# State-space rounds of a hybrid decoder step: inputs and outputs moved on chip instead of through DRAM, tables loaded a round earlier, and the low part moved from GpSimd to VectorE

## The reference

```
u  = h.reshape(L, 64 groups, 16)                 # h = rmsnorm(x)
bu = einsum('gpc,blgc->blgp', bb, u)             # complex, 64 states a group
st = associative_scan(lambda-bar, bu)            # along the 1024 rows
y  = Re(einsum('gcp,blgp->blgc', c, st)) + d * u
y  = gelu(y)
pg = y @ w_glu
out = pg[:, :1024] * sigmoid(pg[:, 1024:])
```

## Time and profile before

| what | value |
|---|---|
| median of 3 runs | 3394.28 us (3385.55 to 3394.67) |
| profiled execution | 3400.61 us |
| its span, first to last instruction | 3398.8 us |
| PE busy | 3170.3 us, 93% |
| DVE, POOL, ACT busy | 1908.5, 869.8, 810.2 us |
| mean granted TensorE clock | 0.96 of full |
| the S5 rounds, from the end of the norm to the first unit of the gate product | 2227 to 2422 us |

### The profile page before, as it was taken

The page is one execution under the profiler, slowest core; times in us unless marked ns, Lnnn a source line. Parts: engine busy times, 40 slices in busy tenths (PEclk is TensorE's granted clock), DMA queues, the critical chain, the costliest instruction groups (busy, mean ns, idle before and its releaser), DMA issues.

```text
span 3398.8 us, 69059 instructions
## 1 busy us (share of the span) xinstructions
PE 3170.3 (93%) x29883; PEld 2989.3 (88%) x29883; DVE 1908.5 (56%) x4225; ACT 810.2 (24%) x1839; POOL 869.8 (26%) x775
## 2 busy tenths in 40 slices
PE   5999999999999999799999999965897999999998
PEld 4879888888888897699999999954897999999997
DVE  5556666666666666587777676376124332333235
ACT  3334444343444343310011100122103100000001
POOL 2202121121212121133333333234231333333331
PEclk8879999999999999899999999977898999999999
DMA  2111222121212111111222222366110111111111
GB/s 97 52 52 54 71 62 62 59 65 53 65 56 68 60 59 61 30 44 53 77 85 71 71 85 73 111 184 185 52 46 25 50 44 51 44 50 44 50 44 63
DMA packets 111326, 223.46 MB, mean 66 GB/s; under 512 B 24880, under 2 KB 59184, under 8 KB 110000
## 3 DMA queue, kind: packets, MB, share of 16 engines
q1 hardware_dynamic: 82400, 177.66, 16.9%
q10 hardware_dynamic: 28624, 41.38, 3.7%
HBM read 177.86 MB, written 41.14 MB: 64 GB/s over the span
## 4 chain that ended last, share of the span: by engine, by line
PE 86%; DVE 9%; ACT 2%; DMA 1%; issue 1%; POOL 1%; SPq 1%; POOLq 0%; DVEq 0%; ACTq 0%
PE ps L223 33%; PE ps L618 16%; PE ps L1361 15%; PE ps L704 5%; PE ps L652 2%; PE ps L239 1%; PE ps L282 1%; PE ps L679 1%; PE ps L645 1%; PE ps L672 1%; PE ps L630 1%; PE ps L685 1%; PE ps L636 1%; DMA tab<-keep_tab 1%; PE ps L1952 1%
## 5 line engine op out<-in xcount | busy, mean ns | idle before, releaser
L223 PE MATMUL ps<-hhi,whi 128*128 128x344 f32 x2376 | 762.7, 321 | 7.3 <-DVE hlo L334 4.2
L223 PE MATMUL ps<-hhi,wlo 128*128 128x344 f32 x2376 | 760.1, 320 | 0.0
L223 PE MATMUL ps<-hlo,whi 128*128 128x344 f32 x2376 | 759.3, 320 | 0.0
L2187 POOL TENSOR_TENSOR wtick<-wtick 128x1 f32<-128x1 f32 x213 | 52.0, 244 | 2345.6 <-PE ps L223 782.9
L2190 POOL TENSOR_TENSOR wlo<-wraw,whi 128x1024 fp32r<-128x1024 f32 x213 | 531.7, 2496 | 17.1
L223 PEld LDWEIGHTS ps<-hhi,whi 128*128 128x128 f32 x2376 | 447.7, 188 | 10.4 <-DVE hlo L334 4.8
L223 PEld LDWEIGHTS ps<-hhi,wlo 128*128 128x128 f32 x2376 | 447.5, 188 | 0.0
L223 PEld LDWEIGHTS ps<-hlo,whi 128*128 128x128 f32 x2376 | 447.0, 188 | 0.1
L618 PE MATMUL ps<-hhi,whi 128*128 128x344 f32 x1152 | 384.7, 334 | 1.8 <-DVE tg L1044 1.8
L618 PE MATMUL ps<-hhi,wlo 128*128 128x344 f32 x1152 | 368.8, 320 | 0.0
L618 PE MATMUL ps<-hlo,whi 128*128 128x344 f32 x1152 | 368.2, 320 | 0.0
(11 more groups left out here) (389 smaller groups left out, 5221.2 us busy)
## 6 DMA issues: line engine op xcount, KB each, us to landing
wraw<-in_w SPq DMA_DIRECT2D x213, 512.0 KB, 3.5
dwork<-keep_rows SPq DMA_DIRECT2D x64, 256.0 KB, 3.6
S<-in_sin ACTq DMA_DIRECT2D x16, 512.0 KB, 3.8
drw<-keep_del SPq DMA_DIRECT2D x32, 256.0 KB, 3.3
out_sout<-S ACTq DMA_DIRECT2D x16, 512.0 KB, 2.7
tab<-keep_tab SPq DMA_DIRECT2D x6, 1088.0 KB, 6.9
keep_u<-hraw SPq DMA_DIRECT2D x8, 580.0 KB, 3.8
uu<-keep_u SPq DMA_DIRECT2D x8, 580.0 KB, 6.8
```

The source lines that it names most:

```text
L223: ins = nc.tensor.matmul(out, w, r[:, kt, blk(n)], start=k == 0, stop=k == 3 * KT - 1)
L2187: G.tensor_tensor(wtick[:, 1:2], wtick[:, 0:1], wtick[:, 0:1], ALU.add)
```

## The change

Both DRAM round trips go. `inputs(r)` becomes eight DMAs from `hs` straight to `uu`, and the eight DMAs of y write `yl` straight away. That leaves y in another order of channels on the partitions (channel within group first), so the rows of the gate weights are fetched in that order. `scaled(kt)` now waits until the input of tile kt-2 is in `uu`. Tables get five places, the first three rounds are loaded early, and rounds 3 and 4 ahead of round 0; from round 5 on a table is issued ahead of the y of round r. The low part goes from POOL to DVE, where `low(r-2)` stands in round r between the products and the scans. `scaled(5)`, `(6)`, `(7)` go behind rounds 1, 2, 3. PE's `ahead` is one round later.

```diff
         def s5_early(s):
-            sp.wait_ge(ee_kept, 16 * 2)
+            sp.wait_ge(ee_kept, 16 * 3)
...
-            for r in range(2):
+            for r in range(3):
                 s5_tables(s, r)
+                s5_powers(s, r)
...
         def s5_sync(s, more_weights):
             def inputs(r):
                 if r >= 3:
                     s.after("PE", f"y{r - 3}.1")
-                sp.wait_ge(u_store[r], 16)
-                sp.dma_start(uu[r % 3][:, :, :], keep_u[r].rearrange("(g c) j n -> (c j) g n", c=G16)).then_inc(uu_in[r], 16)
+                s.after("DVE", f"hs{r}")
+                for g in range(2 * PQ):
+                    sp.dma_start(uu[r % 3][:, g, :], hs[r % 2][G16 * g:G16 * (g + 1), :, :]).then_inc(uu_in[r], 16)
...
-            store_u(0)
-            store_u(1)
             inputs(0)
-            store_u(2)
-            inputs(1)
             s.after("POOL", "zero")
             samples(0)
             samples(1)
-            store_u(3)
-            s5_tables(s, 2)
-            store_u(4)
+            inputs(1)
+            s5_tables(s, 3)
+            s5_powers(s, 3)
             inputs(2)
+            s5_tables(s, 4)
             more_weights()
             for r in range(SR):
-                for kt in ((5, 6), (7,))[r] if r < 2 else ():
-                    store_u(kt)
                 if 3 <= r + 2 < SR:
                     inputs(r + 2)
                 if r == 1:
-                    s5_tables(s, 3)
+                    s.after("DVE", "xp0")
+                    s5_powers(s, 4)
+                if 5 <= r + 2 < SR:
+                    s.after("DVE", f"xp{r - 1}")
+                    if r + 2 == SR - 1:
+                        s.after("DVE", f"hs{KT - 1}")
+                    s5_tables(s, r + 2)
+                    s5_powers(s, r + 2)
                 s.after("ACT", f"ge{r}")
+                if r:
+                    s.after("ACT", f"hi{r - 1}")
+                    s.after("DVE", f"lo{r - 1}")
                 for j in range(STEP):
-                    sp.dma_start(keep_y[r].rearrange("(g c) j n -> j c g n", c=G16)[j], yg[G16 * j:G16 * (j + 1), :, :]).then_inc(y_store, 16)
+                    sp.dma_start(yl3[:, j, :], yg[G16 * j:G16 * (j + 1), :, :]).then_inc(y_in, 16)
                 if r + 2 < SR:
-                    if r + 2 >= 4:
-                        s5_tables(s, r + 2)
                     samples(r + 2)
                 s.after("POOL", f"sto{r}")
                 sp.dma_start(dr["s5o"][r], sto[r % 2][:, :, :, :]).then_inc(s5_out[r % 2], 16)
-                if r:
-                    s.after("ACT", f"hi{r - 1}")
-                    s.after("POOL", f"lo{r - 1}")
-                sp.wait_ge(y_store, 16 * STEP * (r + 1))
-                sp.dma_start(yl, keep_y[r].rearrange("p j n -> p (j n)")).then_inc(y_in, 16)
...
         def s5_dve(v):
             def scaled(kt):
                 if kt >= 2:
-                    v.e.wait_ge(u_store[kt - 2], 16)
+                    v.e.wait_ge(uu_in[kt - 2], 16 * 2 * PQ)
...
+            def low(r):
+                v.after("ACT", f"hi{r}")
+                if r == 1:
+                    v.after("PE", "y1.1")
+                yt = yl3[:, :, 0:NBLK].rearrange("p j c -> p c j")
+                lt = hlo[:, r, 0:T].rearrange("p (c j) -> p c j", j=STEP)
+                ht_ = hhi[:, r, 0:T].bitcast(F32).rearrange("p (c j) -> p c j", j=STEP)
+                v.go(V.tensor_tensor(lt, yt, ht_, ALU.subtract))
+                v.go(V.tensor_tensor(hlo[:, r, T:N], yl3[:, 0, NBLK + 1:XC], hhi[:, r, T:N].bitcast(F32), ALU.subtract), f"lo{r}")
...
                 v.go(V.tensor_tensor(r1[:, 1], r1[:, 1], r2[:, 1], ALU.subtract), f"s{r}.1")
+                if r >= 2:
+                    low(r - 2)
...
-                for kt in ((5, 6), (7,))[r] if r < 2 else ():
-                    scaled(kt)
+                if 5 <= r + 4 < KT:
+                    scaled(r + 4)
                 v.after("DVE", f"xp{r}")
-            v.after("ACT", f"hi{SR - 1}")
-            low_y(v, V, SR - 1)
+            low(SR - 2)
+            low(SR - 1)
...
         def s5_pe(p):
                 outer(r)
-                if r >= 2:
+                if r >= 3:
                     for n in range(2):
-                        ahead(0, n, (r - 2,))
+                        ahead(0, n, (r - 3,))
             for n in range(2):
-                ahead(0, n, (KT - 2,))
+                ahead(0, n, (KT - 3,))
             p.after("ACT", f"vv{SR - 1}")
-            ahead(0, 2, range(KT - 1))
-            for n in range(2):
-                ahead(1, n, range(KT - 1))
+            ahead(0, 2, range(KT - 2))
+            ahead(1, 0, range(KT - 2))
             p.after("ACT", f"ge{SR - 1}")
-            ahead(1, 2, range(KT - 1))
+            for n in (1, 2):
+                ahead(1, n, range(KT - 2))
+            for j in range(2):
+                for n in range(NC3):
+                    ahead(j, n, (KT - 2,))
...
         def s5_act(a):
             def outer(r):
                 if r:
-                    a.e.wait_ge(y_store, 16 * STEP * r)
+                    a.e.wait_ge(y_in, 16 * STEP * r)
...
-                    sp.dma_start(wraw[:, k % 2, :], dr["w"][stream[k]]).then_inc(w_loaded[k % 2], 16)
+                    rows = dr["w"][stream[k]]
+                    if unit_base["glu"][0] <= stream[k] < unit_base["ffn1"][0]:
+                        rows = rows.rearrange("(g c) n -> c g n", c=G16)
+                    sp.dma_start(wraw[:, k % 2, :], rows).then_inc(w_loaded[k % 2], 16)
```

More of the change, by code:

```diff
@@ L90, in build @@
         out_state = sem("out_state")
-        u_store = [sem(f"u_store{k}") for k in range(KT)]
         wt_in = [sem(f"wt_in{r}") for r in range(SR)]
@@ L100, in build @@
         kk_kept = sem("kk_kept")
-        y_store = sem("y_store")
         y_in = sem("y_in")
@@ L1533, in build @@
         EEW, HSW = 2 * PQ * NBLK, STEP * UC
-        early = [hraw[:, r, (r + 1) * N:(r + 1) * N + TABW + EEW] for r in range(2)]
-        tabs5 = [early[r][:, 0:TABW] if r < 2 else (tab0, tab1)[r % 2][:, :] for r in range(SR)]
-        ees5 = [early[r][:, TABW:TABW + EEW].rearrange("p (a q n) -> p a q n", a=2, q=PQ) if r < 2 else (ee0, tmp)[r % 2][:, :, :, :] for r in range(SR)]
+        CHW = TABW - TWT
+        e_a, e_b = hraw[:, 0, 0:TWT + CHW + EEW], hraw[:, 1, 0:EEW + TWT + CHW]
+        e_c, e_d = hraw[:, 0, TABW + EEW:TABW + EEW + CHW], hraw[:, 1, TABW + EEW:TABW + 2 * EEW + TWT]
+        tab_a = (e_a[:, 0:TWT], e_a[:, TWT:TABW])
+        tab_b = (e_b[:, EEW:EEW + TWT], e_b[:, EEW + TWT:EEW + TABW])
+        tab_c = (e_d[:, 0:TWT], e_c)
+        tab_d, tab_e = ((t_[:, 0:TWT], t_[:, TWT:TABW]) for t_ in (tab0, tab1))
+        tabs5 = [tab_a, tab_b, tab_c, tab_d, tab_e, tab_c, tab_d, tab_e]
+        ee_a, ee_b, ee_c = (t_.rearrange("p (a q n) -> p a q n", a=2, q=PQ) for t_ in (e_a[:, TABW:TABW + EEW], e_b[:, 0:EEW], e_d[:, TWT:TWT + EEW]))
+        ee_d = ee0[:, :, :, :]
+        ees5 = [ee_a, ee_b, ee_c, ee_d, ee_a, ee_c, ee_d, tmp]
         hs = [hraw[:, k, KT * N - HSW:KT * N].rearrange("p (j n) -> p j n", j=STEP) for k in range(2)]
-        wtl = [t_[:, 0:TWT].rearrange("p (a q n) -> p a q n", a=2, q=PQ) for t_ in tabs5]
-        cpl = [t_[:, TWT:TWT + TCP].rearrange("p (a q k c) -> p a q k c", a=2, q=PQ, c=G16) for t_ in tabs5]
-        htl = [t_[:, TCP + TWT:TABW].rearrange("p (g n) -> p g n", n=P) for t_ in tabs5]
+        wtl = [t_[0].rearrange("p (a q n) -> p a q n", a=2, q=PQ) for t_ in tabs5]
+        cpl = [t_[1][:, 0:TCP].rearrange("p (a q k c) -> p a q k c", a=2, q=PQ, c=G16) for t_ in tabs5]
+        htl = [t_[1][:, TCP:CHW].rearrange("p (g n) -> p g n", n=P) for t_ in tabs5]
         yl = ab[:, :, :].rearrange("p a n -> p (a n)")[:, 0:STEP * XC]
@@ L1732, in table_act_drain, with s5_powers @@
             A.dma_start(keep_tab[r, :, TWT:TWT + TCP], cp[:, :, :, :, :].rearrange("p a q k c -> p (a q k c)")).then_inc(cp_kept, 16)
+        def s5_powers(s, r):
+            s.e.dma_start(ees5[r], keep_ee[r]).then_inc(tab_in[r], 16)
         def s5_tables(s, r):
             sp = s.e
[L1736 to L1743, removed]
+            sp.dma_start(tabs5[r][0], keep_tab[r, :, 0:TWT]).then_inc(wt_in[r], 16)
+            sp.dma_start(tabs5[r][1], keep_tab[r, :, TWT:TABW]).then_inc(tab_in[r], 16)
         def s5_early(s):
@@ L1749, in s5_early @@
             s.begin("s5", 0)
-            sp.wait_ge(ee_kept, 16 * 2)
-            sp.wait_ge(cp_kept, 16 * 2)
-            sp.wait_ge(wt_kept, 16 * 2)
-            sp.wait_ge(kk_kept, 32 * STEP * 2)
-            for r in range(2):
+            sp.wait_ge(ee_kept, 16 * 3)
+            sp.wait_ge(cp_kept, 16 * 3)
+            sp.wait_ge(wt_kept, 16 * 3)
+            sp.wait_ge(kk_kept, 32 * STEP * 3)
+            for r in range(3):
                 s5_tables(s, r)
+                s5_powers(s, r)
         def s5_sync(s, more_weights):
@@ L1772, in samples @@
```

(15 more changed lines are left out.)

3 lines of the change are left out of this document (removed).

## The result

The changed kernel takes 3426.01 us, the median of 4 runs (3423.53 to 3431.85), against 3393.93 before. The ratio is 1.0094 with a 95% interval of 1.0077 to 1.0111: slower, by 26 to 38 us. The forecast was 3428. The profiled execution took 3423.53, its span is 3421.8.

What follows compares the result with a forecast made beforehand. In the state-space rounds PE waited 8.84 us for a table issued behind SP's y issues; removing that, start +9.2, rounds +29.1 and end -4.4 gave +33.9, so 3434.5 profiled and 3428 median, range 3405 to 3441.

Steps and rivals of the forecast that it cites:

- What is next after the table's wait: State-space rounds: outer, gelu, high part, low part and scans run in series, a turn of 23.6 us at the low clock.
- The closing list: Signs to look for: six waits of 8 to 11 us, turns of 23.6, slow outers, round 0 near 2251.
- I take the low clock: PE's outer products after an idle gap run at granted clock 0.50, 11.4 us each instead of 6.7.
- the second rival: PE's clock rises part way through outer, 8.7 us, saving 2.7 in seven of them: +15, 3409; chance 0.10.
- The wait for the high part: VectorE's low part stands waiting 8 to 11 us for ACT's high part in six of eight rounds.
- The start: Before round 0, scaled waits for inputs to land in uu, so round 0 begins at 2251.5, 9.2 us late.
- Rounds 0 to 7: From round 0's start to xp7 takes 167.8 us for 138.7, 29.1 longer, with four last turns of 23.6.
- The end: From xp7 to PE's last lead product takes 33.0 us for 37.4, a gain of 4.4.
- Sum: Whole kernel: 9.2 + 29.1 - 4.4 = 33.9 us slower, 3434.5 for the profiled execution, 3428 for the median.
- Rival 4: Rounds: SP and PE alone set the turn, the high part's wait costs nothing; 14 us a turn, 3364; chance 0.06.

Runs made afterwards that it cites:

- e3_both: Changed kernel with low(r-2) moved behind xp(r) and, on SP, inputs(r+3) issued ahead of the move of y; 0.9965 of the kernel before.
- e12_fill_best: e8_tab_first with the first three inputs' issues split over SP and ScalarE, table 3 behind inputs(2), and 14 unused matmuls a round before outer; 0.9926.
- e10_tab_late: e8_tab_first with table 3 and its powers issued behind inputs(2) instead of ahead of it; 0.9951 of the kernel before.
- e8_tab_first: e3_both with the tables of round r+2 issued on SP ahead of inputs(r+3); 0.9952 of the kernel before.

## Why the prediction was right

- **What is next after the table's wait.** The step that carried the forecast was that `low(r-2)` ahead of the scans puts outer, gelu, high, low and scans in series. It holds: the turn of rounds 5 to 6 is 23.16 us of the six terms added, each within 0.3 of the one predicted. (The closing list names the low part L1863, its line in the kernel before; here it is L1873.) The trace of the changed kernel alone shows it; e3_both shows that taking it away is worth more than its own size once SP's order is also mended. In the turns to xp3 and xp4 the prediction saw the other loop too, the waits of `scaled` for inputs, but took it to be hidden. In the turn to xp3 it set the pace (nothing waited for the high part), in that to xp4 it was hidden by 1.6 us only, and e3_both shows what it bounds once VectorE's wait is gone.
- **The clock.** "I take the low clock" was right for three outers of seven (11.4 us), and for the other four the second rival was (8.0 to 9.1): the clock rose part way, 3.6 to 6.1 us after outer began. (That rival's "5 us into the inner product" misreads its row: PE's timeline of the kernel before has that inner product begin at 2363.01, so the rise came 4.1 us after PE started, as outer began.) The old trace had two such outers, and both had stayed low, which was too small a sample for a rule. The turns of rounds 2 to 7 were 22.2, 23.2, 20.9, 23.2 and 23.1, for 23.6. That the gap before outer brings the low clock holds: e12_fill_best fills the gaps, and six outers of six run at the full clock; the last section counts all traces. What lifts the clock again within outer stays open.
- **The wait for the high part.** The closing list forecast six waits of 8 to 11 us. There were 8.7, 10.9 and 11.0 in rounds 5 to 7, none in rounds 2 and 3 and 1.6 in round 4. In 2 and 3 the working had said so, since `scaled(6)` and `(7)` come late; the closing list forgot it.
- **The start.** Forecast 9.2 us late, measured 12.0. The term that was off is the cost of eight issues: 3.7 by the rows of y to DRAM, 5.1 to 5.8 here. The first two inputs alone took 3.1 us more of SP than forecast, and table 3 went out that much later. That the tables ahead of inputs(2) matter too was right: inputs(2) landed 10.1 us after table 3's first issue, for 9.7 forecast, and e10_tab_late puts 4 to 5 us on it.
- **Rounds 0 to 7.** Forecast 167.8 from round 0 to xp7, measured 161.5. Of the 6.3 us, 4.0 lie in the last four turns (2.7 of them in the one whose outer rose), 1.5 in the turn to xp3, where the wait for the high part of a slow outer did not come, and 0.8 before xp2. xp2 was forecast 49.7 after the start and came at 48.9, by two errors that cancel: outer(0) rose and took 3.0 less, and the sixteen issues of y(0) and inputs(3) took 11.4 for 7.4. scaled(5) waited 14.73 us for inputs(3) as worked out.
- **The end.** Forecast 33.0, measured 28.8: outer(7) rose on the way (8.0 us) and the lead products then ran at the full clock from the first; PE then waited 1.5 us for the low part of the last tile, which the forecast had hidden. The 37.4 taken for the kernel before is 38.3 by its rows, as the last of those products ended at 2419.3.
- **Sum.** +12.0 + 22.8 - 9.5 = +25.3 for +33.9 forecast. Three terms erred, by 2.8, 6.3 and 5.1, and the first worked against the others; the medians moved by 32. The closeness of 3428 to 3426 is in part luck: the profiled pair alone differs by 22.9 us.
- **Rival 4** (14 us a turn, faster) did not come true and was not a possible outcome of this change, but it is close to what the rounds can do: e3_both and e8_tab_first have turns of 15.7 and 14.5 in the mean and end below the kernel before.

What the change set out to do is sound by these runs: loading tables a round ahead did end the 8.84 us wait, and on chip the moves of y work. The order of the work spoilt it: in the rounds the places of the low part and of the inputs (44 us by e3_both), at the start eight issues on one queue and a table ahead of inputs(2).

## What to carry to other kernels

When a long wait is taken out, write out the next loop on every engine before believing the gain: follow the instruction behind which others queue, and ask what it waits for in the round before. Work that nobody needs soon goes behind the work that feeds the longest chain, on the engine and on the DMA queue alike; which engine does it (2.0 or 2.9 us here) matters less than where it stands. If undoing one suspect gives little, undo two together: 0.3% and 0.4% singly were 1.3% in a pair.

## What the runs showed of the hardware

- What PE did before a float32 outer product (64x128 and 128x128 matmuls with 137 columns, 6.25 us at the full clock, 11.3 at half) goes with its clock. The thirteen traces have 104 of them. Of the 54 that began within 1.13 us of PE's last work none lost the full clock, and where the inner product before had been at 0.50, it rose within 2 us. Of the nine that began 1.73 to 3.71 us after it, all began at the full clock and eight lost it within 1.6 us, with PE busy; the one behind 2.23 us kept it. The 41 that began 4.3 us or more after it all began at 0.50. This one of e3_both had an idle gap of 1.98 us before it:

```profile
2297.40:2298.80 1.40, 1.34 (x12) 1.24 (x12) 1.40 (x1) 0.00 (x0) 0.00 (x0) 0.87 0.44 179
2298.80:2307.90 9.10, 9.10 (x38) 6.75 (x37) 9.10 (x20) 0.00 (x0) 0.00 (x0) 0.50 0.49 71
```

- An outer that begins at 0.50 may or may not rise. Of those 41, 19 stayed there for 11.3 us of unbroken work and 22 rose on the way, after 3.6 to 7.5 us. The length of the gap doesn't tell them apart: in the changed kernel gaps of 6.58, 8.18 and 10.56 us went before the ones that stayed, 6.74, 9.95, 10.27 and 16.37 before the ones that rose. What does tell them apart was not settled.
- A move from 16 partitions of SBUF to 128 partitions costs SP about 0.63 us an issue (5.06 for eight in e3_both, up to 6.29 for the first y of the changed kernel), the same pieces of y to DRAM 0.46 (3.67 for eight). Eight of them set the pace twice in this kernel.
